# Splitting the operand waits of a three-pass matmul: high-high passes first, then low-high, then high-low

## The chip, the cores and the metric

The kernel runs on one NeuronCore of one Trainium2 chip. The metric is the device time of one execution in microseconds (us), the median of several runs. TensorE does the matmuls and has two sides in the profile: PE, the matmuls, and PEld, the loads of the stationary operand, which overlap them. VectorE is DVE, ScalarE is ACT, GpSimd is POOL, SyncE is SP.

## What is computed

The reference runs two decoder layers in float32 on `x` of 256 tokens by 1024 channels. Cut to what matters:

```python
for l in range(2):
    h = rmsnorm(x, norm_mix[l])
    qa, ka, va, qb, kb, vb, qi, ki, wi, qc, kc, vc, g = _split(h @ w_in[l], IN_SIZES)   # 1024 x 5316
    # three mixers: stick-breaking, top-k sparse, sliding window -> o_a, o_b, o_c
    merged = gates[..0] * (o_a @ w_pa[l]) + gates[..1] * (o_b @ w_pb[l]) + gates[..2] * (o_c @ w_pc[l])
    x = x + merged @ w_out[l]
    x = x + cross_attention(rmsnorm(x, norm_x[l]), rmsnorm(mem, norm_mem[l]),
                            w_xq[l], w_xkv[l], w_xo[l], qn_x[l], kn_x[l])
    hf = rmsnorm(x, norm_ffn[l])
    if l % 2 == 0: x = x + swiglu(hf, w_gu_dense[0], w_down_dense[0])         # 2816 wide
    else:          x = x + moe_swiglu(hf, w_router[0], w_gu_moe[0], w_down_moe[0])  # top 2 of 8, 3584 wide
```

Nearly all the arithmetic is in the products with weights.

## The kernel before

**Three passes.** A float32 operand is split in two float32r halves: the high half is a rounded copy made by ScalarE (`act_split` L379 for weights, `act_hi` L485 for activations), the low half the difference, made by VectorE (`dve_split` L385, `dve_lo` L492). A product `h @ w` is then hi x w_hi + lo x w_hi + hi x w_lo, three matmuls into the same PSUM bank. `pe_products` (L499) writes them out: for each 128-row chunk of the contraction, high-high (L504), low-high (L505), high-low (L506). Activations are stationary (128 x 128), weights stream (128 x 512).

**Slots.** Weights come in slots of 128 x 2048 numbers (1 MB; some have half of that), each loaded into one of three `raw` buffers, split by ScalarE into `w_hi` and by VectorE into `w_lo`, and read by TensorE. A slot of 4 chunks by 512 columns is 12 matmuls for each 128-row tile of activations; there are two row tiles in the layers and the dense part and one for an expert. A slot of the `pa` and `pb` projections has 2 chunks. Semaphores order it: `hi_done` and `lo_done` count the slots split, `mm_done` the slots that TensorE has finished. ScalarE waits for `mm_done` before it writes a `w_hi` buffer again, VectorE for `hi_done`, SyncE for `lo_done` before it loads into a `raw` buffer, and TensorE for `lo_done` at the start of each slot (L511, L603, L621, L731, L745). In the gate columns of the input projection the weights are used unsplit in float32 (`pe_gates`, L569).

**Activations.** Before a projection whose input is new (the memory, the normalised inputs "mix", "x" and "ffn", the merged rows "mrg"), TensorE transposes it (`pe_turn` L458), VectorE applies the gain (`dve_gain`, L482), ScalarE writes `hT_hi` (L490, semaphore `..._H`) and VectorE `hT_lo` (L495, `..._L`), each in two halves of 4 chunks. TensorE waits for `..._L` of a half before the slot that uses it (L534, L642, L763). The queue of each engine is in program order: VectorE drains a finished block out of PSUM (L1484, L945, L1664, L579) only after the low halves of up to three slots ahead (`ahead`, L413, and `dve_linear`, L537), where the program puts them first.

**Feed-forward.** The dense part has 11 chunks of 256 hidden channels, an expert has 14, and there are 8 experts, 112 expert chunks in all; both run in loops whose wait values are computed in registers. A chunk is two gate/up slots and one down slot. Between them ScalarE applies the SiLU, VectorE the product, TensorE transposes (L616, L716), ScalarE writes `aT_hi` (L683, L828) and VectorE `aT_lo` (L699, L893). The down slot waits for `lo_done` and for `aT_split`, which says that `aT_lo` is there (L621 and L622, L745 and L746). It has two output halves of 2 chunks each.

**Order of a layer on TensorE** (`pe_program`, L1156): memory keys, input projection, mixers with the gate columns in between, `pa`, `pb`, `pc`, merge, `out`, `xq`, cross attention, `xo`, feed-forward.

## Time and profile before

| | us |
|---|---|
| median of 3 runs (lowest to highest) | 1960.74 (1956.84 to 1961.72) |
| the profiled execution | 1955.1 |
| its span, first to last instruction | 1953.5 |
| busy: PE / PEld / DVE / ACT | 1754.0 / 1348.9 / 1377.2 / 1059.5 |
| L504, L505, L506 with hT, 1488 matmuls each | 610.6 / 597.3 / 596.6 busy |
| L504, L505, L506 with aT, 536 matmuls each | 213.6 / 212.7 / 212.7 busy |
| mean granted TensorE clock | 0.96 of full |

The busy times of PE are of overlapping matmuls whose ends are modelled; what counts is the distance between starts. The layers take the first 370 us and the stretch from 568 to 950, the dense part of layer 0 the time between, the experts the rest.

### The profile page before, as it was taken

To read this page: it belongs to the slowest core of one execution; us is meant where nothing else is said; L and a number is where in the kernel's file an instruction comes from. 1 tells how busy PE (TensorE), PEld (TensorE's weight loads), DVE (VectorE), ACT (ScalarE), POOL (GpSimd) and SP (SyncE) were. 2 spreads that over 40 slices of the span, in tenths; PEclk is the share of its full clock that TensorE was granted. 3 is DMA by queue.
4 is the path that set the end of the run, shared out by engine and by line. 5 is a ranking of instruction groups with operands and counts; after the bars stand their busy time and mean duration, and the time that the engine had idled before them with its cause. 6 is when DMAs were issued, how large, how long until landed. Compare 5 with 4: busy or idle time off the path is not lost.

```text
span 1953.5 us, 21775 instructions
## 1 busy us (share of the span) xinstructions
PE 1754.0 (90%) x7553; PEld 1348.9 (69%) x7553; DVE 1377.2 (70%) x1288; ACT 1059.5 (54%) x967; POOL 49.8 (3%) x69
## 2 busy tenths in 40 slices
PE   6796878799989968886499999999999999999995
PEld 5653466688867634665388887888888888888884
DVE  6447467554456464674488888888888888888884
ACT  4212434434343224243377777777777777777773
POOL 2100000000000000000100000000000000000000
PEclk9898989899989989897799999999999999999997
DMA  8821259255435312440699999999999999999993
GB/s 240 266 91 63 82 194 363 103 194 190 175 127 175 109 66 82 178 177 22 233 355 370 376 367 371 371 371 373 367 376 369 366 381 365 376 368 365 382 363 137
DMA packets 74813, 502.80 MB, mean 257 GB/s; under 512 B 8524, under 2 KB 9356, under 8 KB 18320
## 3 DMA queue, kind: packets, MB, share of 16 engines
q1 hardware_dynamic: 65712, 466.55, 62.6%
q0 software_dynamic: 8656, 34.57, 5.7%
q10 hardware_dynamic: 400, 1.08, 0.1%
q8 instruction: 28, 0.46, 0.1%
q14 instruction: 17, 0.14, 0.0%
HBM read 483.55 MB, written 18.61 MB: 257 GB/s over the span
## 4 chain that ended last, share of the span: by engine, by line
PE 76%; DVE 10%; ACT 6%; DMA 3%; issue 2%; DVEq 2%; POOL 0%; ACTq 0%; SPq 0%; POOLq 0%
PE ps L504 23%; PE ps L505 23%; PE ps L506 23%; DMA raw<-in_layer_tiles 3%; PE ps L569 2%; DVE w_lo L388 2%; PE ps L716 1%; ACT scratch L1259 1%; ACT w_hi L383 1%; DVE scratch L1386 1%; DVE st L1357 1%; DVEq L1360 1%; DVE scratch L1436 1%; DVE st L1440 1%; DVE hT_lo L495 1%
## 5 line engine op out<-in xcount | busy, mean ns | idle before, releaser
L504 PE MATMUL ps<-w_hi,hT_hi 128*128 128x512 f32 x1488 | 610.6, 410 | 57.9 <-DVE hT_lo L495 24.1
L505 PE MATMUL ps<-w_hi,hT_lo 128*128 128x512 f32 x1488 | 597.3, 401 | 0.0
L506 PE MATMUL ps<-w_lo,hT_hi 128*128 128x512 f32 x1488 | 596.6, 401 | 0.0
L884 DVE TENSOR_TENSOR w_lo<-raw,w_hi 128x2048 fp32r<-128x2048 f32 x168 | 385.0, 2292 | 69.4 <-ACT w_hi L820 69.4
L884 DVE TENSOR_TENSOR w_lo<-z,w_hi 128x2048 fp32r<-128x2048 f32 x168 | 384.5, 2290 | 51.7 <-ACT w_hi L820 48.6
L504 PEld LDWEIGHTS ps<-w_hi,hT_hi 128*128 128x128 f32 x1488 | 285.1, 192 | 130.4 <-DVE w_lo L388 30.0
L820 ACT ACTIVATE w_hi<-z 128x2048 fp32r<-128x2048 f32 x168 | 321.6, 1915 | 40.6 <-PE ps L506 34.7
L820 ACT ACTIVATE w_hi<-raw 128x2048 fp32r<-128x2048 f32 x168 | 321.0, 1911 | 24.3 <-PE ps L506 24.3
L506 PEld LDWEIGHTS ps<-w_lo,hT_hi 128*128 128x128 f32 x1488 | 285.3, 192 | 68.9
L505 PEld LDWEIGHTS ps<-w_hi,hT_lo 128*128 128x128 f32 x1488 | 285.6, 192 | 62.4
L388 DVE TENSOR_TENSOR w_lo<-raw,w_hi 128x2048 fp32r<-128x2048 f32 (+1 forms) x89 | 194.6, 2194 | 126.9 <-ACT w_hi L383 126.2
L383 ACT ACTIVATE w_hi<-raw 128x2048 fp32r<-128x2048 f32 (+1 forms) x89 | 162.6, 1834 | 199.7 <-PE ps L506 128.9
L504 PE MATMUL ps<-w_hi,aT_hi 128*128 128x512 f32 x536 | 213.6, 398 | 3.5 <-DVE aT_lo L893 2.0
L506 PE MATMUL ps<-w_lo,aT_hi 128*128 128x512 f32 x536 | 212.7, 397 | 0.0
L505 PE MATMUL ps<-w_hi,aT_lo 128*128 128x512 f32 x536 | 212.7, 397 | 0.0
L569 PE MATMUL ps<-raw 128*128 128x512 f32 (+1 forms) x384 | 158.4, 570 | 26.4 <-DVE z L579 26.4
L569 PEld LDWEIGHTS ps<-raw 128*128 128x128 f32 x384 | 72.7, 197 | 107.5 <-issue 107.2
L504 PEld LDWEIGHTS ps<-w_hi,aT_hi 128*128 128x128 f32 x536 | 100.9, 188 | 31.4 <-issue 5.5
L506 PEld LDWEIGHTS ps<-w_lo,aT_hi 128*128 128x128 f32 x536 | 101.1, 189 | 24.5
L505 PEld LDWEIGHTS ps<-w_hi,aT_lo 128*128 128x128 f32 x536 | 101.0, 188 | 23.7
L828 ACT ACTIVATE aT_hi<-ps 128x256 fp32r<-128x256 f32 x112 | 43.2, 385 | 107.9 <-PE ps L716 107.9
L824 ACT ACTIVATE headsT<-ps 128x256 f32<-128x256 f32 x112 | 42.9, 383 | 65.4 <-PE ps L506 65.4
(235 smaller groups left out, 1015.8 us busy)
## 6 DMA issues: line engine op xcount, KB each, us to landing
z<-in_moe_tiles SPq DMA_DIRECT2D x168, 1024.0 KB, 4.9
raw<-in_moe_tiles SPq DMA_DIRECT2D x168, 1024.0 KB, 4.8
raw<-in_layer_tiles SPq DMA_DIRECT2D x68, 1024.0 KB, 4.9
raw<-in_dense_tiles SPq DMA_DIRECT2D x33, 1024.0 KB, 4.8
rows_of_experts<-z POOLq DMA_DIRECT2D x1, 8704.0 KB, 44.2
z<-in_b_gate POOLq DMA_DIRECT2D x4, 1536.0 KB, 11.4
z<-rows_of_experts POOLq DMA_DIRECT2D x9, 512.0 KB, 8.2
raw<-in_layer_tiles SPq DMA_DIRECT2D x8, 512.0 KB, 3.9
```

Source lines behind the costliest of these rows:

```text
L383: act.activation(w_hi[:, ring, 0:width], raw[:, ring, 0:width], ACT.Copy).then_inc(sem("hi_done"), 1)
L388: v.tensor_tensor(w_lo[:, ring, 0:width], raw[:, ring, 0:width], w_hi[:, ring, 0:width].bitcast(F32), ALU.subtract).then_inc(sem("lo_done" ...
L495: v.tensor_tensor(hT_lo[:, ks, :], src[:, ks, :], hT_hi[:, ks, :].bitcast(F32), ALU.subtract) \
L504: pe.matmul(acc, a, wh, start=start and j == 0, stop=False)
L505: pe.matmul(acc, b, wh, start=False, stop=False)
L506: ins = pe.matmul(acc, a, wl, start=False, stop=stop and last)
L569: ins = pe.matmul(ps[:, LIN + i, 0:n], gate_x(l)[:, kk, i * P:(i + 1) * P], w[:, k, :], start=kk == 0, stop=kk == KC - 1)
L716: ins = pe.transpose(ps[:, 6, f * P:(f + 1) * P], a_sb[:, 0, f * P:(f + 1) * P], ident)
L820: act.activation(w_hi[:, ring, :], moe_raw(p), ACT.Copy).then_inc(sem("hi_done"), 1)
L824: act.activation(silu_sb[:, 0, :], ps[:, bank, 0:FC], ACT.Silu).then_inc(sem("silu"), 1)
L828: act.activation(aT_hi[:, :, 0:P], psA(1), ACT.Copy).then_inc(sem("aT_hi"), 1)
L884: v.tensor_tensor(w_lo[:, ring, :], moe_raw(p), w_hi[:, ring, :].bitcast(F32), ALU.subtract) \
```

## The change

`pe_products` runs all high-high passes of the chunks of a slot, then all low-high, then all high-low, for one row tile at a time. Two optional waits stand inside: `x_lo` (the low half of the activations) before the low-high passes and `w_lo_v` (`lo_done`) before the high-low ones. The callers pass them for the first row tile (or the first output half) of a slot alone. The waits at the start of a slot become waits for the high halves: `hi_done` for `lo_done`, `..._H` for `..._L`, `aT_hi` for `aT_split`. The waits for `oT_L` before `pa` and for `xo_L` before `xo` stay.

```diff
-        def pe_products(pe, acc, hk, wk, start, stop, hi=hT_hi, lo=hT_lo):
+        def pe_products(pe, acc, hk, wk, start, stop, hi=hT_hi, lo=hT_lo, x_lo=None, w_lo_v=None):
 
-            for j, ((k, cols), (wh, wl)) in enumerate(zip(hk, wk)):
-                a, b = hi[:, k, cols], lo[:, k, cols]
-                last = j == len(hk) - 1
-                pe.matmul(acc, a, wh, start=start and j == 0, stop=False)
-                pe.matmul(acc, b, wh, start=False, stop=False)
-                ins = pe.matmul(acc, a, wl, start=False, stop=stop and last)
+            for j, ((k, cols), (wh, _)) in enumerate(zip(hk, wk)):
+                pe.matmul(acc, hi[:, k, cols], wh, start=start and j == 0, stop=False)
+            if x_lo is not None:
+                pe.wait_ge(sem(x_lo[0]), x_lo[1])
+            for (k, cols), (wh, _) in zip(hk, wk):
+                pe.matmul(acc, lo[:, k, cols], wh, start=False, stop=False)
+            if w_lo_v is not None:
+                pe.wait_ge(sem("lo_done"), w_lo_v)
+            for j, ((k, cols), (_, wl)) in enumerate(zip(hk, wk)):
+                ins = pe.matmul(acc, hi[:, k, cols], wl, start=False, stop=stop and j == len(hk) - 1)
             return ins
 
-        def pe_block_slot(pe, ring, kcs, n, k0, lo_v, first, final, blk_v):
-
-            pe.wait_ge(sem("lo_done"), lo_v)
+        def pe_block_slot(pe, ring, kcs, n, k0, lo_v, first, final, blk_v, x_lo=None):
+
+            pe.wait_ge(sem("hi_done"), lo_v)
...
-                                  [(wh[:, k, :], wl[:, k, :]) for k in range(kcs)], first, final)
+                                  [(wh[:, k, :], wl[:, k, :]) for k in range(kcs)], first, final,
+                                  x_lo=x_lo if i == 0 else None, w_lo_v=lo_v if i == 0 else None)
...
+                    x_lo = None
                     if h_ready and b == b0:
-                        pe.wait_ge(sem(h_ready), 2 * l + h + 1)
+                        pe.wait_ge(sem(h_ready + "_H"), 2 * l + h + 1)
+                        x_lo = (h_ready + "_L", 2 * l + h + 1)
...
             def down(c, s, ring, first, last):
-                pe.wait_ge(sem("lo_done"), s + (1 - N_GATE))
-                pe.wait_ge(sem("aT_split"), c + 1)
+                pe.wait_ge(sem("hi_done"), s + (1 - N_GATE))
+                pe.wait_ge(sem("aT_hi"), c + 1)
...
-                                          hi=aT_hi, lo=aT_lo)
+                                          hi=aT_hi, lo=aT_lo, x_lo=("aT_split", c + 1) if i + h == 0 else None,
+                                          w_lo_v=s + (1 - N_GATE) if i + h == 0 else None)
...
-                pe.wait_ge(sem("ffn_L"), half + 1)
-                gate_up(0, half)
+                pe.wait_ge(sem("ffn_H"), half + 1)
+                gate_up(0, half, x_lo=("ffn_L", half + 1))
...
-        def pe_moe_gate_up(pe, par, k, ring, bank, lo_v):
-            pe.wait_ge(sem("lo_done"), lo_v)
+        def pe_moe_gate_up(pe, par, k, ring, bank, lo_v, x_lo=None):
+            pe.wait_ge(sem("hi_done"), lo_v)
...
-            pe.wait_ge(sem("hg_L"), n + 1)
+            pe.wait_ge(sem("hg_H"), n + 1)
```

The dense gate/up slots, the expert down slot and the calls of `pe_linear` for "mem", "mix", "mrg" and "x" are changed in the same way.

## Rows read from the trace of the kernel before

**Rows 1.** Page, part 4: the chain that ended last, by engine.
```profile
PE 76%; DVE 10%; ACT 6%; DMA 3%; issue 2%; DVEq 2%; POOL 0%; ACTq 0%; SPq 0%; POOLq 0%
```

**Rows 2.** Windows: stretch, length, busy us (instructions) of PE, PEld, DVE, ACT, POOL, granted clock, DMA.
```profile
965.30:1928.80 963.50, 961.50 (x4270) 773.25 (x4271) 841.25 (x563) 713.40 (x568) 7.46 (x14) 1.00 0.94 364
605.46:608.87 3.41, 3.41 (x9) 2.64 (x10) 1.43 (x5) 3.34 (x5) 0.00 (x0) 0.50 0.06 26
```

**Rows 3.** Timeline, a slot boundary in the expert loop: start us, us, engine, line.
```profile
1498.33 2.29 DVE L884 TENSOR_TENSOR w_lo<-raw,w_hi 128x2048 fp32r<-128x2048 f32 x1 [0.67 <-ACT w_hi L820]
...
1501.28 0.19 PEld L504 LDWEIGHTS ps<-w_hi,hT_hi 128*128 128x128 f32 x1
1501.51 0.40 PE L504 MATMUL ps<-w_hi,hT_hi 128*128 128x512 f32 x1
...
1501.74 0.40 PE L505 MATMUL ps<-w_hi,hT_lo 128*128 128x512 f32 x1
```

**Rows 4.** Timeline, second slot of `pa`, layer 0; brackets: idle before, releaser.
```profile
255.89 1.22 DVE L388 TENSOR_TENSOR w_lo<-raw,w_hi 128x1024 fp32r<-128x1024 f32 x1
...
257.17 0.69 PE L504 MATMUL ps<-w_hi,hT_hi 128*128 128x512 f32 x1 [2.10 <-DVE w_lo L388]
257.66 0.63 PE L505 MATMUL ps<-w_hi,hT_lo 128*128 128x512 f32 x1
258.08 0.63 PE L506 MATMUL ps<-w_lo,hT_hi 128*128 128x512 f32 x1
```

**Rows 5.** Chain in order of time, layer 0, start: start us, us, what.
```profile
40.32 22.80 DMA raw<-in_layer_tiles
```

**Rows 6.** Chain in order of time, first projections of layer 0.
```profile
263.93 4.75 DMA raw<-in_layer_tiles
```

**Rows 7.** Timeline of ACT and DVE, first projections of layer 0.
```profile
262.06 1.91 ACT L383 ACTIVATE w_hi<-raw 128x2048 fp32r<-128x2048 f32 x1 [3.04 <-DMA raw<-in_layer_tiles]
...
262.67 4.56 DVE L388 TENSOR_TENSOR w_lo<-raw,w_hi 128x1024 fp32r<-128x1024 f32 x3 [0.16 <-issue]
...
270.65 2.29 DVE L388 TENSOR_TENSOR w_lo<-raw,w_hi 128x2048 fp32r<-128x2048 f32 x1 [0.58 <-ACT w_hi L383]
```

**Rows 8.** Chain in order of time, output projection of layer 0.
```profile
299.33 4.49 DVE w_lo L388 x2
```

**Rows 9.** Timeline of DVE, drains of the query projection, layer 0 and layer 1.
```profile
333.66 0.75 DVE L1664 TENSOR_SCALAR scratch<-ps,st 128x512 f32<-128x512 f32 x1 [1.65 <-PE ps L506]
...
873.86 1.61 DVE L1664 TENSOR_SCALAR scratch<-ps,st 128x512 f32<-128x512 f32 x2
```

**Rows 10.** Timeline, start of the dense part, and input projection of layer 1.
```profile
371.25 2.36 DVE L495 TENSOR_TENSOR hT_lo<-scratch,hT_hi 128x1024 fp32r<-128x1024 f32 x2
...
372.53 0.50 PE L504 MATMUL ps<-w_hi,hT_hi 128*128 128x512 f32 x1 [2.72 <-DVE hT_lo L495]
...
605.29 0.67 PE L504 MATMUL ps<-w_hi,hT_hi 128*128 128x512 f32 x1 [2.40 <-DVE hT_lo L495]
```

**Rows 11.** Timeline of PE, start of the input projection of layer 0.
```profile
46.38 0.50 PE L504 MATMUL ps<-w_hi,hT_hi 128*128 128x512 f32 x1 [2.41 <-DVE hT_lo L495]
```

**Rows 12.** Timeline of PE, memory keys of layer 1 and first expert.
```profile
575.89 0.79 PE L504 MATMUL ps<-w_hi,hT_hi 128*128 128x512 f32 x1 [3.29 <-DVE hT_lo L495]
...
953.02 0.80 PE L504 MATMUL ps<-w_hi,hT_hi 128*128 128x512 f32 x1 [2.37 <-DVE hT_lo L898]
```

**Rows 13.** Timeline, second chunk of the first expert.
```profile
962.94 4.49 DVE L884 TENSOR_TENSOR w_lo<-raw,w_hi 128x2048 fp32r<-128x2048 f32 x2 [1.38 <-ACT w_hi L820]
...
965.29 0.50 PE L504 MATMUL ps<-w_hi,hT_hi 128*128 128x512 f32 x1 [1.58 <-DVE w_lo L884]
...
967.35 0.42 DVE L893 TENSOR_TENSOR aT_lo<-ps,aT_hi 128x256 fp32r<-128x256 f32 x1
```

**Rows 14.** Timeline, last down slot of the kernel.
```profile
1926.84 0.38 ACT L828 ACTIVATE aT_hi<-ps 128x256 fp32r<-128x256 f32 x1 [0.83 <-PE ps L716]
...
1928.82 0.48 PE L504 MATMUL ps<-w_hi,aT_hi 128*128 128x512 f32 x1 [2.01 <-DVE aT_lo L893]
```

More of the change, by code:

```diff
@@ L598, in pe_dense, with gate_up @@
         def pe_dense(pe, s0, n):
-            def gate_up(c, half):
+            def gate_up(c, half, x_lo=None):
                 s, ring = c * 3 + (s0 - 1 + half), place[s0 + 2 + half]
@@ L608, in gate_up @@
                     ins = pe_products(pe, ps[:, 4 + i, :], [(4 * half + k, cols) for k in range(4)],
-                                      [(wh[:, k, :], wl[:, k, :]) for k in range(4)], half == 0, half == 1)
+                                      [(wh[:, k, :], wl[:, k, :]) for k in range(4)], half == 0, half == 1,
+                                      x_lo=x_lo if i == 0 else None, w_lo_v=s + (1 - N_GATE) if i == 0 else None)
                 ins.then_inc(sem("mm_done"), 1)
@@ L717, in pe_turn_chunk, with pe_moe_down @@
             ins.then_inc(sem("aT_turned"), 1)
-        def pe_moe_down(pe, first, last, ring=None):
+        def pe_moe_down(pe, first, last, lo_v, aT_v, ring=None):
             ring = moe_ring(2) if ring is None else ring
+            pe.wait_ge(sem("hi_done"), lo_v)
+            pe.wait_ge(sem("aT_hi"), aT_v)
             wh = w_hi[:, ring, :].rearrange("p (k n) -> p k n", k=2)
@@ L726, in pe_moe_down @@
                                   [(wh[:, f, cols], wl[:, f, cols]) for f in range(2)], first, last,
-                                  hi=aT_hi, lo=aT_lo)
+                                  hi=aT_hi, lo=aT_lo, x_lo=("aT_split", aT_v) if h == 0 else None,
+                                  w_lo_v=lo_v if h == 0 else None)
             ins.then_inc(sem("mm_done"), 1)
-        def pe_moe_gate_up(pe, par, k, ring, bank, lo_v):
-            pe.wait_ge(sem("lo_done"), lo_v)
+        def pe_moe_gate_up(pe, par, k, ring, bank, lo_v, x_lo=None):
+            pe.wait_ge(sem("hi_done"), lo_v)
             wh = w_hi[:, ring, :].rearrange("p (k n) -> p k n", k=4)
@@ L734, in pe_moe_gate_up, with pe_moe_chunk @@
             pe_products(pe, ps[:, bank, :], [(4 * k + q, col_of(par)) for q in range(4)],
-                        [(wh[:, q, :], wl[:, q, :]) for q in range(4)], k == 0, k == 1).then_inc(sem("mm_done"), 1)
-        def pe_moe_chunk(pe, ip, par, u, d):
+                        [(wh[:, q, :], wl[:, q, :]) for q in range(4)], k == 0, k == 1, x_lo=x_lo, w_lo_v=lo_v) \
+                .then_inc(sem("mm_done"), 1)
+        def pe_moe_chunk(pe, ip, par, u, d, x_lo=None):
             off, coff, c = at(ip, par, MOE), at(ip, par, N_MOE), u * 2 + d
             static = isinstance(c, int)
-            pe_moe_gate_up(pe, par, 0, moe_ring(0), 4 + d, off + (u * 6 + (3 * d + SPL0)))
+            pe_moe_gate_up(pe, par, 0, moe_ring(0), 4 + d, off + (u * 6 + (3 * d + SPL0)), x_lo)
             pe.wait_ge(sem("act_done"), coff + (c + N_DENSE))
@@ L1169, in pe_program @@
                         .then_inc(sem("dist_ps"), 1)
-                pe_linear(pe, "xkv", l, nblk=1, h_ready="mem_L")
+                pe_linear(pe, "xkv", l, nblk=1, h_ready="mem")
                 if l == 0:
```

22 lines of the change are left out of this document (9 added, 13 removed).

## The prediction

> **What bounds the kernel now.** I read the shares of the chain that ended last first: 76% of it is TensorE, 10% VectorE, 3% a transfer [rows 1]. That share is not one thing, so the windows by stretch came next. From 965 to 1929 us, half of the run, TensorE is busy for 961.5 of 963.5 us at the full clock [rows 2]. There each matmul starts 0.23 us after the one before [rows 3], so a weight slot of 12 matmuls lasts 2.8 us, and the half that the change delays its wait for is ready early: one w_lo ends at 1500.62, and the slot that reads it starts its weight load at 1501.28 [rows 3]. TensorE is the bound, it waits for nothing, and the order of its passes leaves the number of its matmuls alone. The dense feed-forward of layer 0 looks the same. What the change can win lies in the rest, where the timeline shows TensorE standing before a matmul whose last releaser is a subtraction: hT_lo (L495, L898), w_lo (L388, L884) or aT_lo (L699, L893). I looked at each of these places for two things: when the high half was ready, and what comes after.
>
> **What a stall gives back.** TensorE now starts a slot when both halves of both operands are there. After the change it starts when the high halves are there, does 4 high-high matmuls (2 where the contraction has two chunks), then asks for the low half of the activations, does as many low-high ones, then asks for w_lo. Despite the change's title this runs one row tile at a time: only the passes of row tile 0 stand before the waits. So a stall on hT_lo is covered by at most 4 matmuls, 4 x 0.233 = 0.93 us at the full clock, or 1.7 us at half clock, where starts are 0.42 us apart [rows 4]; nor can more be won than the subtraction lasts. I now go through them in time.
>
> Layer 0, first 68 us (two stalls on hT_lo, the second before 46.38): nothing. The chain runs there through a weight transfer issued at 40.32 that takes 22.8 us [rows 5], and before it through ScalarE's and VectorE's own work.
>
> First projection after the mixers (once per layer): the second slot starts at 257.17 after 2.10 us idle, released by a w_lo that began, with w_hi done, at 255.89 [rows 4]. Two high-high and two low-high matmuls fit in the 1.28 us. They save 0.93 us at the full clock and up to 1.7 at half. That reaches the path: the drain of this slot, the next w_lo and the transfer issued at 263.93 hang on it [rows 6]. A cap comes from VectorE: the third of its next three subtractions needs a w_hi that ends at 262.06 + 1.91 = 263.97 (now it starts at 262.67 + 4.56 - 2.29 = 264.94), and the later w_lo at 270.65 has 0.58 us of idle before it [rows 7], so 0.97 + 0.58 = 1.55 us at most. I take 1.3 in each of two layers: **2.6**. The stall on w_lo before the slot behind it gives nothing: TensorE waits again later for drains that follow that transfer.
>
> Output projection (hT_lo, both layers): nothing. TensorE would start 0.93 us sooner, but the chain leaves it here: from hT_lo over the key statistics and the logarithm and exponential on ScalarE to two subtractions of 4.49 us [rows 8], behind which the drain of the finished block is queued on VectorE.
>
> Query projection (hT_lo): in layer 0 the last drain starts after 1.65 us of idle, in layer 1 the two drains run back to back, 1.61 us together [rows 9]; VectorE is the bound of the second to within 0.1 us. So **1.65** at most in layer 0, 0 in layer 1.
>
> Dense feed-forward, layer 0: hT_hi is ready at 371.25, TensorE starts at 372.53 [rows 10]: 0.93 saved. Layer 1, normalised input at 605.29: the same 0.93. Both stand in front of an unbroken run of TensorE.
>
> Clock. In four places a stall is followed by 3.41 us at a granted clock of 0.50 (one is shown, that of the layer-1 input, [rows 2]; the others are in the first projection, the query projection and the dense part of layer 0). In 3.41 us at 0.427 us apiece 8 matmuls start, which take 1.87 us at the full clock: a stretch costs 1.55 us. A stall with 0.9 us of work put into it may not bring the clock down; the one before 46.38, with 2.41 us idle, did not, for the first matmul after it lasts 0.50 us, not 0.69 as at 257.17 [rows 4, 11]. I count half, 0.77, for the dense and for the layer-1 input: **1.7 each**; the query projection's is in its 1.65.
>
> Memory keys of layer 1 (575.89, idle 3.29) and first expert (953.02, idle 2.37) start at half clock [rows 12]. hT_lo takes 1.22 us, all of which the high-high passes (1.7 us) fill. That is 1.2 us if the clock comes up as much sooner as TensorE starts, 1.2 x 0.233/0.427 = 0.66 if it comes up when it does now, and 2.8 if it comes up one such 3.41-us stretch sooner. I take **1.2** and **0.9**.
>
> First expert, 965.29: idle 1.58 us for a w_lo whose w_hi was done at 962.94 [rows 13]. The 8 matmuls ahead of the new wait (1.87 us) cover all of it, but the down slot behind it then meets aT_lo, which stands behind VectorE's two subtractions of 4.49 us and ends at 967.77 [rows 13]. TensorE would start at 965.29 - 1.58 = 963.71, reach that slot at 966.5, do its 2 high-high matmuls and wait; then 10 matmuls from 967.8 end 0.8 us sooner than 12 from 963.71 + 1.58 + 2.9 = 968.2 do now: **0.8**.
>
> aT_lo before the last down slot of the dense part and of the kernel: 2 high-high matmuls fit in between aT_hi, at the second done at 1926.84 + 0.38 = 1927.22, and the start at 1928.82 [rows 14]: **0.9** for both.
>
> Sum: 2.6 + 1.65 + 1.7 + 1.7 + 1.2 + 0.9 + 0.8 + 0.9 = 11.5 us. With every term at its lower bound (1.9 + 0.9 + 0.9 + 0.9 + 0.7 + 0.7 + 0 + 0.9) it is 6.9, at its upper (3.1 + 1.65 + 2.5 + 2.5 + 2.8 + 1.3 + 1.6 + 0.9) 16.4. The profiled execution took 1955.1 us around a span of 1953.5, so it would take 1943.6. The median of the runs is 5.6 us above that execution, and I take the gain off the median: 1960.7 - 11.5 = **1949.2 us**.
>
> **What it adds.** One more wait on TensorE per weight slot, two more in a down slot (for the two halves of aT), and the arithmetic for their values in the loops. Queued behind each is only TensorE's own stream; ScalarE waits for its end to reuse w_hi, SyncE for VectorE's subtractions, whose order is unchanged. No DMA moves. A slot already begins with a wait, and a met one shows no gap: 1501.28, 1501.51, 1501.74 run on at 0.23 across the boundary [rows 3]. The new wait for w_lo stands 8 matmuls later (1.87 us), so it is met 0.66 + 1.87 = 2.5 us ahead. I cost it at zero; the cover is this lead. The Trainium skill ("TensorE: Matmul & The Clock Gate", section "Step-by-step: what each phase is for") has weight loads pulled ahead of the matmuls in flight. By that the sum stays as it is as long as a met wait doesn't stop it, of which the page says nothing; if it did, each new wait would lay a load bare, which is the second rival. Below zero isn't possible, since TensorE's rate in the expert loop is that of its matmuls. The bound above zero is that rival's 45 to 85 us.
>
> **Rivals.** (1) *The saved time is lost downstream.* Twice above VectorE's fixed chain already took all of it. If that also holds in the layer-1 input, the query projection and the first projection, what is left is dense, aT, memory and expert starts at their lower bounds: 0.9 + 0.9 + 0.7 + 0.7 = 3.2 us, 1957.5 us. For: VectorE is in nearly every chain of the layers. Against: in the timeline it idles for TensorE at those places. (2) *A wait inside the stream costs although it is met*: the next weight load can't be started under the matmul before. The loads take 0.19 us and start one matmul ahead [rows 3]; the first matmul after a stall lasts 0.50 instead of 0.40 [rows 3, 13], so 0.10 each is exposed. There are 112 expert chunks (8 experts by 14), with 4 waits inside the slots of each (two gate/up slots one each, the down slot two): 448 x 0.10 = 45 us, less 11, gives 1994 us, and with the full 0.19 load 2034. It decides as soon as TensorE's instruction stream is read less than one matmul ahead. For it: no row of before has a wait between two passes of a slot. Against: the present waits at slot starts, also in front of a weight load, show none of it. (3) *The clock helps everywhere*: no half-clock stretch is left after any stall, and the starts come a step sooner: the upper sum, 16 us or a little more, 1943 us. (4) The order is what the diff says, but the waits are met in the same order as before because ACT's high half is late rather than VectorE's low half: excluded, since at each stall above the high half is earlier by at least its subtraction's 0.4 to 2.3 us.
>
> **How the numbers follow.** Forecast 1949 (6.9 to 14 us won): 0.66. Rival 3: 0.12. Rival 1: 0.17. Rival 2: 0.05. What a measurement of this kernel can tell from no change is about 0.3%, 5.9 us. Faster by more: the forecast, rival 3 and a little of rival 1, 0.79; within it: the rest of rival 1, 0.16; slower 0.05. The range for 8 in 10 takes in rival 3 and the better part of rival 1: 1941 to 1957.
>
> **What would show it.** Right: L504 starts released by ACT hT_hi or w_hi at the stalls, L505 (low-high) by DVE hT_lo with about 0.3 us of idle, the expert stretch of 963.5 us the same to within 1, and the same starts 0.23 us apart. Shorter stalls with the drains at the old distance would show rival 1; starts over 0.23 apart at a change of pass inside the expert loop, rival 2. The prediction is wrong at its root if the expert stretch changes at all by more than its first 3 us.

## The result, and the profile after

The changed kernel took 1938.8 us (median of 4 runs, 1937.5 to 1940.4) beside 1961.2 us of the kernel before (4 runs, 1956.8 to 1962.0): a ratio of 0.989, 95% interval 0.9874 to 0.9905. The forecast was 1949.2 us with a range of 1941 to 1957. The sign was right and the size was not: the time is outside the range by 2 us. Run again with more executions beside it, the change took 1937.6 against 1956.9 us, ratio 0.9895 [0.9880, 0.9909], so 19 to 22 us. In these medians one execution of each kernel, of some 3550 us, is left out as slow. The four runs of before on record lie high, for the same kernel had medians of 1956.7 to 1956.9 us in four later sessions.

The profiled execution of after took 1940.4 us around a span of 1938.7; that of before 1955.1 around 1953.5. The two traces differ by 14.8 us, and that difference is what can be followed row by row. It is less than that of the medians, because the profiled execution of after was the slowest of its four and that of before was quicker than all four of its runs. Line numbers have moved: the three passes are now L502 (high-high), L506 (low-high) and L510 (high-low). First the page of after: the shares of its chain, and the three passes with the idle time just before them.

```profile
PE 76%; DVE 10%; ACT 6%; DMA 3%; issue 2%; DVEq 2%; POOL 0%; ACTq 0%; SPq 0%; POOLq 0%
...
L502 PE MATMUL ps<-w_hi,hT_hi 128*128 128x512 f32 x1488 | 426.8, 408 | 42.2 <-DVE z L586 13.2
L506 PE MATMUL ps<-w_hi,hT_lo 128*128 128x512 f32 x1488 | 414.9, 400 | 1.4 <-DVE hT_lo L495 0.9
L510 PE MATMUL ps<-w_lo,hT_hi 128*128 128x512 f32 x1488 | 413.2, 399 | 3.2 <-DVE w_lo L388 3.2
```

The shares are the same as in [rows 1]; they don't show the change at all. The idle times do: in front of the low-high pass with hT 1.4 us are left in the whole kernel (and 1.5 with aT), in front of the high-low pass 3.2. The busy column can't be set beside that of before: it counts overlapping matmuls of one line once, and in after four matmuls of one line follow each other. The mean length of one matmul, 408, 400 and 399 ns, is within 2 ns of before's 410, 401 and 401. The waits of TensorE say what this replaced. Of the kernel before (in its second profiled execution, span 1953.3), the rows with a subtraction's result as the releaser; columns are total us, times, longest:

```profile
PE ps L504 <- DVE hT_lo L495: 23.1, 11, 3.5
PE ps L504 <- DVE w_lo L388: 8.5, 4, 2.2
PE ps L504 <- DVE hT_lo L898: 2.4, 1, 2.4
PE ps L504 <- DVE aT_lo L893: 2.0, 1, 2.0
PE ps L504 <- DVE w_lo L884: 1.6, 1, 1.6
PE ps L504 <- DVE aT_lo L699: 1.5, 1, 1.5
```

The same view of after, every row of the three passes with a half of an operand as the releaser:

```profile
PE ps L502 <- ACT hT_hi L490: 10.0, 9, 2.6
PE ps L510 <- DVE w_lo L388: 3.2, 4, 1.2
PE ps L502 <- DVE hT_lo L495: 2.8, 2, 1.4
PE ps L506 <- DVE aT_lo L902: 1.5, 2, 0.8
PE ps L502 <- ACT hT_hi L841: 1.1, 1, 1.1
PE ps L502 <- ACT w_hi L383: 1.1, 2, 0.6
PE ps L506 <- DVE hT_lo L495: 0.9, 1, 0.9
PE ps L502 <- ACT aT_hi L692: 0.8, 1, 0.8
PE ps L502 <- ACT aT_hi L837: 0.6, 1, 0.6
```

Before, these waits sum to 39.1 us; after, to 22.0. That is 17.1 us less. All waits of TensorE together fell from 178.8 to 164.7 us, 14.1 less, while the span fell by 14.6: over the whole kernel nearly all of the gain is idle time of TensorE, and 3.0 us of the 17.1 came back in front of other matmuls. The busy time is 1753.5 us, and it was 1754.5. This balance holds for the sum only: in single stages the time in matmuls changed by up to 5 us, in both directions, through the clock.

The expert loop, which the prediction called full, became a little shorter, and the waits in it cost nothing. Windows of after from the second chunk of the first expert to the last down slot, then a stretch in the layer-1 input and one in the output projection of layer 0 (columns as in [rows 2]), and in the fence after it the timeline of TensorE over one gate/up slot inside the loop and the turn behind it:

```profile
953.08:1914.81 961.73, 960.32 (x4273) 774.35 (x4272) 841.86 (x563) 715.21 (x570) 7.47 (x14) 1.00 0.94 364
599.24:602.65 3.41, 3.35 (x15) 2.41 (x14) 2.00 (x2) 3.33 (x4) 0.00 (x0) 1.00 0.42 178
302.50:305.91 3.41, 3.41 (x10) 2.62 (x9) 3.11 (x14) 0.00 (x0) 0.00 (x0) 0.50 1.04 437
```

```profile
1324.08 1.09 PE L502 MATMUL ps<-w_hi,hT_hi 128*128 128x512 f32 x4
1325.02 1.09 PE L506 MATMUL ps<-w_hi,hT_lo 128*128 128x512 f32 x4
1325.95 1.09 PE L510 MATMUL ps<-w_lo,hT_hi 128*128 128x512 f32 x4
1326.88 0.38 PE L725 MATMUL ps<-consts,headsT 128*128 128x128 f32 x2
```

The stretch of [rows 2] lasted 963.5 us and lasts 961.7: 1.4 us less between its second chunk and the last turn, 1.4 less in the wait that ends it, and 1.1 more at its start, where TensorE now comes early and waits for aT_lo. The passes follow each other after 0.94, 0.93 and 0.93 us, four matmuls of 0.233 us each, although a wait stands between the second and the third. From 966.6 us to the last turn, all 874 changes of pass in the expert loop, half of them with a wait, are 0.230 to 0.235 us from the start before. In the layer-1 input the granted clock is 1.00 where it was 0.50; in the output projection of layer 0 a stretch at 0.50 stands where before had none.

The places of the sum, in the timeline of after, in order of time: TensorE's first high-high matmul at the dense part, at the memory keys of layer 1 and at the layer-1 input; VectorE's last drains of the query projection of layer 1; the first expert; the last down slot:

```profile
371.43 0.50 PE L502 MATMUL ps<-w_hi,hT_hi 128*128 128x512 f32 x1 [1.46 <-ACT hT_hi L490]
...
571.80 1.80 PE L502 MATMUL ps<-w_hi,hT_hi 128*128 128x512 f32 x4 [2.59 <-ACT hT_hi L490]
...
598.90 1.20 PE L502 MATMUL ps<-w_hi,hT_hi 128*128 128x512 f32 x4 [1.15 <-ACT hT_hi L490]
...
863.33 1.41 DVE L1673 TENSOR_SCALAR scratch<-ps,st 128x512 f32<-128x512 f32 x2
...
941.86 2.07 PE L502 MATMUL ps<-w_hi,hT_hi 128*128 128x512 f32 x4 [1.11 <-ACT hT_hi L841]
...
1916.16 0.74 PE L506 MATMUL ps<-w_hi,aT_lo 128*128 128x512 f32 x2 [0.65 <-DVE aT_lo L902]
```

The idle times of [rows 10, 12] are 0.7 to 1.3 us shorter and are now ended by ScalarE's high half: 2.72 became 1.46, 3.29 became 2.59, 2.40 became 1.15, 2.37 became 1.11. The last row shows where the new order is not enough: two high-high matmuls of a down slot don't fill the time that aT_lo takes, and 0.65 us are left.

### The profile page after: what moved, and what is told of

The parts are those of the page before. It is cut to its first block, busy times and chain, and to the rows that moved or that the text cites. A ratio compares the mean times of both kernels' runs of the same rounds, so it can differ in the third digit from the quotient of the medians.

```text
span 1938.7 us, 21775 instructions
## 1 busy us (share of the span) xinstructions
PE 1753.5 (90%) x7553; PEld 1346.2 (69%) x7553; DVE 1377.0 (71%) x1288; ACT 1059.6 (55%) x967; POOL 49.8 (3%) x69
## 4 chain that ended last, share of the span: by engine, by line
PE 76%; DVE 10%; ACT 6%; DMA 3%; issue 2%; DVEq 2%; POOL 0%; ACTq 0%; SPq 0%; POOLq 0%
PE ps L506 23%; PE ps L510 23%; PE ps L502 23%; DMA raw<-in_layer_tiles 3%; DVE w_lo L388 2%; PE ps L576 2%; PE ps L725 1%; ACT w_hi L383 1%; ACT scratch L1268 1%; DVE scratch L1395 1%; DVE st L1366 1%; PE ps L1160 1%; DVEq L1369 1%; DVE scratch L1445 1%; DVE st L1449 1%
## 5 line engine op out<-in xcount | busy, mean ns | idle before, releaser
L502 PE MATMUL ps<-w_hi,hT_hi 128*128 128x512 f32 x1488 | 426.8, 408 | 42.2 <-DVE z L586 13.2
L506 PE MATMUL ps<-w_hi,hT_lo 128*128 128x512 f32 x1488 | 414.9, 400 | 1.4 <-DVE hT_lo L495 0.9
L510 PE MATMUL ps<-w_lo,hT_hi 128*128 128x512 f32 x1488 | 413.2, 399 | 3.2 <-DVE w_lo L388 3.2
L502 PEld LDWEIGHTS ps<-w_hi,hT_hi 128*128 128x128 f32 x1488 | 271.7, 191 | 105.1 <-issue 22.6
L510 PEld LDWEIGHTS ps<-w_lo,hT_hi 128*128 128x128 f32 x1488 | 282.7, 190 | 73.6 <-DVE w_lo L388 4.9
L506 PEld LDWEIGHTS ps<-w_hi,hT_lo 128*128 128x128 f32 x1488 | 282.5, 190 | 72.9 <-DVE hT_lo L495 5.3
L506 PE MATMUL ps<-w_hi,aT_lo 128*128 128x512 f32 x536 | 168.7, 396 | 1.5 <-DVE aT_lo L902 1.5
L502 PE MATMUL ps<-w_hi,aT_hi 128*128 128x512 f32 x536 | 168.5, 396 | 1.3 <-ACT aT_hi L692 0.8
L510 PE MATMUL ps<-w_lo,aT_hi 128*128 128x512 f32 x536 | 168.4, 396 | 0.0
L506 PEld LDWEIGHTS ps<-w_hi,aT_lo 128*128 128x128 f32 x536 | 100.5, 188 | 26.8 <-DVE aT_lo L902 2.4
L502 PEld LDWEIGHTS ps<-w_hi,aT_hi 128*128 128x128 f32 x536 | 100.5, 188 | 26.0 <-issue 1.8
L510 PEld LDWEIGHTS ps<-w_lo,aT_hi 128*128 128x128 f32 x536 | 100.7, 188 | 24.4
```

The source lines that it names most:

```text
L502: pe.matmul(acc, hi[:, k, cols], wh, start=start and j == 0, stop=False)
L506: pe.matmul(acc, lo[:, k, cols], wh, start=False, stop=False)
L510: ins = pe.matmul(acc, hi[:, k, cols], wl, start=False, stop=stop and j == len(hk) - 1)
```

## The experiments

All ran beside the kernel before on the same chip; a ratio is to those runs. The first four shared 28 runs of before (median 1956.8 us), the next four 16 (1956.9), the next four 21 (1956.8), the last two 23 (1956.7). A gain "by the ratio" is the ratio's share of that median; it differs from the difference of the medians by up to 1.7 us.

**The kernel before again.** No edit.

> The kernel before, unchanged, for a second profile and more times. The change took 22.4 us off the median but only 14.8 us between the two profiled executions, since the profiled one of before (1955.1 us) lay 6 us under the median of its runs. Theory A (the profiled execution of before was a quick one, and executions of one kernel differ by some us through the half-clock stretches of TensorE): ratio 1.000, and a profile of 1957 to 1962 us whose extra time against the first lies in matmul runs at half clock in the two layers, with the expert loop the same to 1 us. Theory B (profiling itself makes before quicker): this profile is again at 1955 us, 5 us or more under the median.

1954.9 us, 12 runs from 1952.8 to 1960.9, ratio 0.9999 [0.9985, 1.0012]. Neither theory came out as written: the profile was again at 1954.9 us, but this time that is the median of its runs. What follows: executions of one kernel lie 8 us apart here, and the 88 of before in the four sessions 11 us (1951.8 to 1962.6), while their work is the same. So a single profile is not the kernel's time, and gains below 3 us are read from many runs or not at all.

**The order alone.** All waits in front of the first pass.

```diff
+            if w_lo_v is not None:
+                pe.wait_ge(sem("lo_done"), w_lo_v)
+            if x_lo is not None:
+                pe.wait_ge(sem(x_lo[0]), x_lo[1])
             for j, ((k, cols), (wh, _)) in enumerate(zip(hk, wk)):
                 pe.matmul(acc, hi[:, k, cols], wh, start=start and j == 0, stop=False)
-            if x_lo is not None:
-                pe.wait_ge(sem(x_lo[0]), x_lo[1])
```

> The pass order of the change (high-high, low-high, high-low), with all waits back in front of the first pass: for both high halves, then the low half of the activations, then that of the weights. Theory A (only the shortened stalls give time, the order costs and gives nothing): 1961 us within 3, ratio 0.998 to 1.002, starts 0.233 us apart in the expert loop. Rival C (the order itself is quicker, for instance at the 112 transposes of the expert loop, whose stretch drifted by 1.4 us between the two profiles): 1 to 8 us quicker than before without any split wait.

1959.1 us (12 runs), ratio 1.0013 [0.9999, 1.0027]: nothing, or up to 5 us lost. The order alone gains nothing, so the gain is in the places of the waits. (This kernel also has one more wait in front of a slot than before; what that does in the expert loop is told further down.)

**The activations' low half late, w_lo early**, and the reverse. In each, one of the two waits stands between the passes and the other in front of them.

> The change with the wait for w_lo back in front of the first pass: only the wait for the low half of the activations (hT_lo, aT_lo) stands between passes. Theory A by its terms: dense 0.9 to 2.5, layer-1 input 0.9 to 2.5, memory 0.7 to 2.8, query projection up to 1.65, first expert 0.9, aT_lo 0.9: 7 us off 1961, so 1954. The prediction under-sized the memory and input terms of layer 1 (4.6 us between the profiles where 2.9 was said), so up to 10 us: 1951 to 1954. Rival D (the w_lo splits give most of the gain): 1956 or more.

1946.0 us (6 runs), ratio 0.9942 [0.9925, 0.9959], 11.4 us by the ratio.

> The change with the wait for the low half of the activations back in front of the first pass: only the wait for w_lo stands between passes. Theory A: first projections (pa to pc) 3.0 us in each of two layers as the profile of after shows there, second chunk of the first expert 0.8 to 1.8: 7 to 8 us off 1961, so 1953 to 1954. With the split of the activations' wait 14 to 18 us in sum, so that the two halves add up to the whole change within 3 us. Rival D (w_lo splits give most): 1945 or less.

1949.6 us (11 runs), ratio 0.9968 [0.9955, 0.9980], 6.3 us by the ratio. Both kernels were faster than what was expected of them, some 4 us of which is that the expectations started from 1961 us. Both halves of the change work by themselves and nearly add up to the whole. The prediction had 3.4 us for the w_lo places (2.6 and 0.8) and 8.1 for the rest; the runs give about 6 and 11. Both parts were sized too small.

**The change again.**

> The change, unchanged, for its ratio with many more runs of both kernels: 28 later runs of before had a median of 1956.8 us, not 1961.2, and the activation split alone gave 11, the weight split alone 7 us. Theory A (the two splits add up, and the 22.4 us of the first comparison held some 4 us of spread of before): 1938 to 1941 us, ratio 0.990 to 0.992. Theory B (the first comparison was right, and the two splits together give more than their sum): 0.989 or less.

1937.6 us, ratio 0.9895 [0.9880, 0.9909]. The gain holds: 19.2 us by the medians, 20.5 by the ratio.

**Unused matmuls in two idle times of the kernel before**, 3.4 us of them in front of the first wait for the activations in the input blocks of layer 1 and in the dense part. No pass is moved.

```diff
+        def pe_fill(pe, bank, n):
+            for _ in range(n):
+                pe.matmul(ps[:, bank, :], ident, consts[:, 0:4, :].rearrange("p i n -> p (i n)"), start=True, stop=True)
...
+                        if name == "in" and l == 1 and h == 0:
+                            pe_fill(pe, 5, 4)
...
+                if half == 0:
+                    pe_fill(pe, 6, 4)
                 pe.wait_ge(sem("ffn_L"), half + 1)
```

> The kernel before, with waits and pass order as they were, and with matmuls added whose results nothing reads: 4 (identity by constants, float32, 128x512, 0.427 us apart at the full clock) in front of the wait of the layer-1 input projection, and 4 in front of the dense part's first wait. They only fill idle time of TensorE. Theory K (half of what a covered stall gives is the half-clock stretch after it, 1.55 us each, which work inside the idle time avoids): the stretches of 3.41 us at half clock from 373 and 605 us are gone and the dense part and the input projection end 1.55 us sooner each: 3 us off, ratio 0.9984 give or take the interval. Theory N (the clock has no part in it, the low-high order hides work only): no change or slower by the added work, 0 to +1 us at these two places.

1956.5 us (12 runs), ratio 0.9992 [0.9983, 1.0001]. Each of these float32 matmuls is two instructions of 0.427 us, 3.4 us in all, where the idle times are 2.7 and 2.4: the filling ends 0.7 to 1 us behind the operand. It cost TensorE that time, and the kernel was no slower, which suggests that something of that size came back. The stretch at half clock at 605 us was gone, the one at 373 stood 12 us later. Since two effects cancel here, the size was set right in a later run.

**Unused matmuls in three longer waits of after** (8.5 us ahead of the first wait of the cross attention, 15.4 us behind the product for the top-k, 4.3 us in the output projection).

> The change plus unused matmuls of the same kind in three long waits of TensorE in each layer: 5 before the second output-projection block, 10 before the wait for the cross-attention probabilities, 18 before the gate columns that wait for the drain during the top-k. Theory K: the half-clock stretches that start in these waits vanish (in the profile of after: 302 in layer 0, 343 and 876 of 10 us, part of 169 and 705), each us of matmuls that ran at half clock costs 0.45 us: 4 to 10 us off the change, 1930 to 1936. Theory N: 1939 or slower, since nothing is gained and a filler that overruns its wait delays the chain.

1946.4 us (6 runs), ratio 0.9950 [0.9934, 0.9966], 9 us slower than after. The granted clock of the profiled execution was the highest of all (0.925 to 0.976 over the six):

```profile
die 0 (median of its cores): 1942.4 us, clock 0.976
```

That is 0.976 where after had 0.96, in a longer span: behind each of the six groups of fillers the next matmul starts with no idle time before it, so the fillers, longer than the waits, stood in the path. A clock that is up is no gain if the way to keep it up stands in the path.

**All row tiles first.** In slots that aren't the last of their block, and in the first dense slot, the high-high pass of both row tiles, then low-high of both, then high-low of both. This is what the change's title says and its code does not.

```diff
+            for acc, hk in zip(accs, hks):
+                for j, ((k, cols), (wh, _)) in enumerate(zip(hk, wk)):
+                    pe.matmul(acc, hT_hi[:, k, cols], wh, start=start and j == 0, stop=False)
+            if x_lo is not None:
+                pe.wait_ge(sem(x_lo[0]), x_lo[1])
+            for acc, hk in zip(accs, hks):
+                for (k, cols), (wh, _) in zip(hk, wk):
+                    pe.matmul(acc, hT_lo[:, k, cols], wh, start=False, stop=False)
+            pe.wait_ge(sem("lo_done"), w_lo_v)
```

> The change as its title says it: in every slot that is not the last of its block (and in the first dense gate/up slot) the high-high passes of both row tiles stand before the low-high passes of both, and those before the high-low ones, so 8 high-high matmuls (1.9 us) stand in front of the wait for hT_lo instead of 4 (0.93 us). hT_lo takes 1.22 us, so each full-clock stall is covered for all of it: 0.3 us more at each of five places (dense, layer-1 input, query projection of layer 0; the memory and output ones give nothing more). Theory A: 1 us off the change, 1938 us within 2. Rival: the second tile's drain wait now stands before all passes, and the slots give back 0.3 to 1 us each: 1940 to 1945.

1950.0 us (5 runs), ratio 0.9956 [0.9943, 0.9969]: 12 us slower than after. The waits of TensorE of this kernel that grew, for the drain of the input blocks, the memory keys and the first projections:

```profile
PE ps L517 <- DVE z L611: 15.7, 8, 9.2
PE ps L517 <- DVE mem_kv L1671: 3.4, 1, 3.4
PE ps L502 <- DVE scratch L1524: 8.9, 4, 3.3
```

A block whose first pass runs over both tiles needs both drains of the previous block before it starts, and VectorE does them one after the other: 8 waits for z instead of 3. In after these rows have 13.2, 0.5 and 7.0 us, 7.3 less together, of the 11.1 us by which the two profiles differ. Row tile by row tile, the second drain is hidden behind the first tile's 12 matmuls.

**Only pa, pb and pc.** The kernel before, with the new order and the late wait for w_lo in these three blocks alone; and its opposite, after with the wait for w_lo in front of the first pass there.

```diff
+            pe.wait_ge(sem("hi_done" if split else "lo_done"), lo_v)
...
+                if split:
+                    ins = pe_products_split(pe, ps[:, LIN + i, 0:n], hk, wk, first, final, lo_v if i == 0 else None)
```

> The kernel before with one part of the change alone: in the blocks pa, pb and pc of both layers TensorE waits for the high half of the weights in front of the first pass and for w_lo in front of the high-low pass, in the new order; everywhere else the code is that of before. The prediction put this part at 2.6 us in all, since VectorE's drain was taken for the cap (1.55 us a layer, 1.3 used). The profiles of before and after show 3.2 and 3.0 us a layer between the start of pa and the end of pc. Theory A (the transfer one slot earlier sets the stage, the cap was wrong, and it is this part alone that does it): 5 to 7 us faster than before, ratio 0.9965 to 0.9975, and in the profile 3.0 us less from the start of pa to merge in each layer, of which some 1.55 us is a stretch at the low clock that is no longer there. Theory B (the prediction's term was right and the rest comes from elsewhere in the change): 2 to 3.5 us faster, ratio about 0.9985.

1950.6 us (10 runs), ratio 0.9970 [0.9959, 0.9980], 5.9 us faster.

> The change without that part: the kernel after, but in pa, pb and pc the wait for w_lo stands in front of the first pass again; all else is after. Theory A of the run before (6 us belong to this part and the parts add up): 1944 to 1946 us beside 1957 of before, ratio 0.9935. Theory B (the part is worth 2.6 us): 1940 to 1941.5, ratio about 0.991.

1943.4 us (6 runs), ratio 0.9933 [0.9916, 0.9950], slower than after by 5.7 us by the medians of the two sessions, 7.4 by the ratios. Both say the same thing from either side: 6 to 7 us for the two layers, where the prediction had 2.6. TensorE's waits for w_lo there, first with the late wait, then without:

```profile
PE ps L508 <- DVE w_lo L388: 3.0, 4, 1.2
```

```profile
PE ps L502 <- DVE w_lo L388: 8.5, 4, 2.2
```

**Fillers that fit.** As above, 1.7 us at each of the two places of before.

> The kernel before with unused float32 matmuls that fit into two waits, 1.7 us each (four instructions of 0.427 us), in front of the first wait for the activations in the input blocks of layer 1 and in the dense layer; the idle times there were 2.4 and 2.7 us, so nothing is overrun. No pass is moved. Theory A (what the change takes from the low clock at these places is a saving of its own, one stretch of 3.41 us at half clock, worth some 1.55 us, for each idle time that gets too short): the stretches at 372 and 605 us are gone and the kernel is 1.5 to 3 us faster than before, ratio 0.9985 to 0.9992. Theory B (the stretches only move to the next short wait): the same as before within 0.5 us, and new stretches at half clock show behind the filled waits.

1954.0 us (12 runs), ratio 0.9980 [0.9969, 0.9992]: 2.8 us by the medians, 1.6 to 6.1 by the interval, faster without a pass or a wait moved. The start of the dense part, in this kernel's timeline:

```profile
372.68 1.88 PE L461 MATMUL ps<-consts 128*128 128x512 f32 x4
375.56 0.50 PE L509 MATMUL ps<-w_hi,hT_hi 128*128 128x512 f32 x1 [1.00 <-DVE hT_lo L500]
375.90 0.40 PE L510 MATMUL ps<-w_hi,hT_lo 128*128 128x512 f32 x1
```

The row behind the first is 0.34 us later, at the full clock. In the kernel before (its second profile) the layer-1 input began like this, with the next row 0.59 us later and then 0.42 us apiece:

```profile
605.49 0.80 PE L504 MATMUL ps<-w_hi,hT_hi 128*128 128x512 f32 x1 [2.41 <-DVE hT_lo L495]
606.08 0.63 PE L505 MATMUL ps<-w_hi,hT_lo 128*128 128x512 f32 x1
606.50 0.63 PE L506 MATMUL ps<-w_lo,hT_hi 128*128 128x512 f32 x1
```

The stretch at half clock behind the wait of the layer-1 input, there in both profiles of before, is gone with fillers and gone with the change, which shortens this idle time by 1.3 us. Over all kernels of this section and both profiles of before and after it is the same: the stretch is there in all six profiles in which this wait stands as before (starting between 601.5 and 606.2 us), and in none of the ten in which the wait is late or filled. The one at the dense part is in the first profile of before and not in the second; of that place alone the profiles prove nothing. At the layer-1 input the stretch is a cost beside the idle time, and an idle time that TensorE partly works through doesn't bring it on.

**Fillers that fit, in the three longer waits of after** (1.7, 4.3 and 7.7 us).

> The kernel after with unused float32 matmuls in three longer waits of each layer, now sized to the idle time: 1.7 us in front of the second output block, 4.3 us in front of the first wait of the cross attention, 7.7 us after the product that is sent to the top-k. Nothing of the computation is changed. Theory A (a stretch at half clock behind a long wait is avoided by keeping TensorE at work in the wait, 1.5 to 3 us each, and the earlier attempt lost only by overrunning the waits): 4 to 9 us faster than after, 1930 to 1935 us beside 1957 of before. Theory B (the time behind these waits is set by VectorE or a transfer, not by TensorE's clock): the same as after within 1 us, 1937 to 1939. Theory C (it still overruns): slower than after, 1940 or more.

1942.5 us (6 runs), ratio 0.9924 [0.9910, 0.9939], still 5 us slower than after: theory C by the number, though not by its reason, for behind each of the six groups of fillers TensorE is idle for 0.4 to 1.5 us more. Its granted clock in the profile:

```profile
die 0 (median of its cores): 1942.5 us, clock 0.964
```

The second profile of after has the same 0.964; over all executions this kernel had 0.964 to 0.969 and after 0.960 to 0.964, so the clock came up by little. Beside that profile of after the time is lost in the mixers with the fillers of the top-k, 3.0 us in layer 0 and 4.2 in layer 1; in layer 0 three stretches at half clock (from 186, 204 and 217 us) stand there that it has not. Another 1.4 us are lost by 74 us, ahead of any filler; behind the other fillers 1.6 and 0.8 us are won in layer 0. Why the stretches came there isn't known. None of the kernels tried beats after.

**The activations' low half late, in two groups.** From the third kernel of this section: first only in layer 1's memory and input blocks and in the dense part, then everywhere else.

```diff
+                        if l == 1 and h_ready in ("mem", "mix"):
                             pe.wait_ge(sem(h_ready + "_H"), 2 * l + h + 1)
                             x_lo = (h_ready + "_L", 2 * l + h + 1)
+                        else:
+                            pe.wait_ge(sem(h_ready + "_L"), 2 * l + h + 1)
```

> The kernel before with the new pass order, and with the wait for the activations' low half late in two groups only: the memory and input blocks of layer 1 and the first two slots of the dense layer. Every other wait stands as before. The prediction's terms for these are 1.2, 1.7 and 1.7 us, 4.6 in all. Theory A (the excess is the half-clock stretches that these idle times bring on): 6 to 7.5 us faster than before, ratio 0.9962 to 0.9969, with no stretch at half clock at 605 us. Theory B (the excess is elsewhere): 4 to 5 us, ratio about 0.9977.

1951.4 us (12 runs), ratio 0.9974 [0.9961, 0.9986], 5.3 us faster than before.

> The complement of the run before: the new pass order, the wait for the activations' low half late in the memory and input blocks of layer 0, the output and query projections of both layers, the starts of the experts and everywhere the gated activation's two halves are used; the memory and input blocks of layer 1, the dense layer's first slots and all waits for w_lo as before. The prediction's terms for these sum to 3.5 us (1.65 query of layer 0, 0.9 start, 0.9 halves). Theory A (these terms were right): 3 to 4.5 us faster than before, ratio 0.9977 to 0.9985, the stretch at half clock at 605 us still there. Theory B: 5 us or more, ratio under 0.9975.

1956.6 us (12 runs from 1947.6 to 1959.8), ratio 0.9998 [0.9985, 1.0010]: no faster than before. The first is nearer to theory B, though the stretch at 605 us is gone as theory A says; the second is below both theories, nothing where 3.5 us were predicted. Its profiled execution is the fastest of its 12, 9 us under their median, so its trace does not stand for its runs. Together the two groups give some 5.5 us, and the whole late wait for the activations gave 11: the parts don't add up, and why isn't shown.

## Why the prediction was off

**What held.** TensorE's rate at the full clock didn't change, the gain over the whole kernel is idle time before matmuls whose last releaser was a subtraction, and a wait that is met costs nothing: rival 2 falls, with the starts 0.23 us apart at every change of pass in the loop. The Trainium skill ("TensorE: Matmul & The Clock Gate", section "Step-by-step: what each phase is for") has weight loads pulled ahead of the matmuls in flight; the trace agrees also with a met wait between them (the load at 948.99 us, its matmul at 949.22, the matmul before them at 948.99), of which the page says nothing. Rival 1 falls for the kernel as a whole: only 3.0 of 17.1 us came back as other waits. The prediction's own sign for the expert stretch, the same to within 1 us, was missed by 0.8 (963.5 and 961.7).

**Place by place**, the difference of the two profiles (what the start of the next stage moved by), with the forecast in brackets: query projection of layer 0 1.7 us (1.65) and of layer 1 0.2 (0; VectorE's drains run back to back in both, [rows 9] and 863.33 above), first expert's second chunk 0.7 (0.8), output projections 0 but for the clock (0). Memory keys of layer 1 2.1 (1.2), layer-1 input 2.5 (1.7), dense part 2.5 (1.7), end of the kernel 2.3 (0.45), down slot of the dense part 0.7 (0.45), first projections 3.2 and 3.0 (1.3 each), expert loop 1.4 (0), start of the first expert 0.3 (0.9). Against them stand losses that no step had: 1.6 us in the output projection of layer 0 and 2.9 and 0.7 in the cross attentions, through half-clock stretches that fell elsewhere, and 0.7 ahead of the first projection. The sum is 14.7, of the profiles' 14.8.

**The step that failed: the half-clock stretches of the first projections, put at nothing.** The prediction saw that TensorE could start 0.9 to 1.7 us sooner there, limited the gain to 1.55 us a layer by VectorE's next subtractions, took 1.3, and added nothing for the clock. Its paragraph on the clock names one stretch at half clock in this stage of layer 0; before had three of them in it in each layer (from 257.3, 264.1 and 274.4 us, and from 800.0, 806.9 and 817.1), and after has one in layer 0 (268.4) and two, one behind the other, in layer 1 (800.8 to 807.7). The waits did what they should (rows of TensorE in the second slot of pa):

```profile
256.42 0.74 PE L502 MATMUL ps<-w_hi,hT_hi 128*128 128x512 f32 x2 [0.58 <-ACT w_hi L383]
257.00 0.63 PE L506 MATMUL ps<-w_hi,hT_lo 128*128 128x512 f32 x2
257.95 0.73 PE L510 MATMUL ps<-w_lo,hT_hi 128*128 128x512 f32 x2 [0.32 <-DVE w_lo L388]
```

Here is the stage from the first matmul of pa to the last of pc, layer 0 and layer 1, first of before, then of after (columns as in [rows 2]; the length less PE's busy time is TensorE's idle time):

```profile
252.03:286.67 34.64, 28.03 (x96) 21.16 (x96) 24.69 (x26) 11.88 (x8) 0.00 (x0) 0.85 0.65 231
794.62:829.28 34.66, 28.03 (x96) 21.10 (x96) 24.69 (x26) 11.99 (x8) 0.00 (x0) 0.85 0.62 229
```

```profile
252.81:284.13 31.32, 25.45 (x96) 18.68 (x96) 24.54 (x26) 11.90 (x8) 0.00 (x0) 0.95 0.70 253
787.01:818.72 31.71, 26.32 (x96) 19.59 (x96) 24.64 (x26) 12.00 (x8) 0.00 (x0) 0.89 0.70 251
```

The idle time fell from 6.6 to 5.9 us and from 6.6 to 5.4: 0.7 and 1.2 us, 2.0 in all, so the cap of 1.55 held and the 2.6 were even a little much. TensorE's waits for w_lo fell by more, from 8.5 to 3.2 us, and the rest of that came back in front of drains and of w_hi: in this stage rival 1 holds in part. The other 4.3 of the 6.3 us are the same 192 matmuls at a higher clock, which had no term. The second profiles of before and after show the same split. The runs with these blocks alone and without them put the part at 6 to 7 us.

How much of this belongs to the late wait? The other kernels show that the stage moves in steps of the stretches. With w_lo asked for in front of the first pass it lasted 34.6 to 34.8 us in ten of 18 cases (nine profiles, two layers each; three stretches), 33.0 to 33.2 in three (two stretches), 31.5 to 31.7 in four (one stretch), and 32.8 in one. With the late wait it lasted 31.2 to 31.7 us in 13 of 14, and 32.7 in the kernel with all row tiles first. One of the four is layer 0 of the first kernel with unused matmuls, whose code up to this point is that of before, pass order and all, since its first filler comes later:

```profile
251.17:282.67 31.50, 25.02 (x96) 18.46 (x96) 24.63 (x26) 11.91 (x8) 0.00 (x0) 0.95 0.70 253
```

It has 6.5 us of idle time, nearly as much as before, and is 3.1 us shorter all the same; the second kernel with unused matmuls, with the same code up to here, took 34.8. So with one stretch in either the late wait is worth 0.2 to 0.3 us in layer 0, and most of its gain in this stage is that the long cases stay away. That the shorter idle times are what keeps them away fits the layer-1 input above, but was not tried in this stage.

**The second: the clock was counted at half.** The terms of the dense part and the layer-1 input had 0.77 us of a possible 1.55 each. Neither stretch is in the profiles of after, and fillers that fit were worth 2.8 us (1.6 to 6.1) at the two places, where 3.1 is two whole stretches and 1.5 was predicted; the interval leaves out 1.5 by a hair only. At the end of the kernel, where before had a stretch at half clock from 1929.8 us on, after has none. Rival 3, which said so everywhere, had too small a number for it and was also not quite right: other stretches appeared, as the one at 302.50.

**The third: the loop was not quite full.** The prediction put nothing on it. In the kernel before (second profile) the down slot of some chunks waits some hundredths of a us for an aT_lo:

```profile
1332.45 0.42 DVE L893 TENSOR_TENSOR aT_lo<-ps,aT_hi 128x256 fp32r<-128x256 f32 x1
...
1332.99 0.45 PE L504 MATMUL ps<-w_hi,aT_hi 128*128 128x512 f32 x1
```

Here aT_lo ends at 1332.87 and the slot begins at 1332.99. 16 of the 112 chunks last 8.65 to 8.79 us instead of 8.61; in after none does. That fits aT_lo being asked for two matmuls later, and is 1.4 us over the loop. With the order alone these chunks last 8.80 to 8.91 us and the loop 2.1 us longer than before. It is not the order that does this: the two last kernels have the same order, and their loops are 0.1 and 1.2 us shorter than that of before. The order alone has four waits in front of a down slot, before and these two have fewer there; that this is the reason is not shown.

**What stays open.** The two groups of the activations' wait give 5 to 6 us less than the whole of it, more than the half width of any one interval (2.4 to 3.3 us). And with w_lo's 6.3 and the activations' 11.4 the whole should be 17.7 us; it is 19.2 by the medians of its second session and 20.5 by the ratio, about the width of the intervals. In the cross attention of layer 0 TensorE was 2.5 us less idle and 5.4 us longer in its matmuls; why the stretches fell there is not known. How the half-clock stretches fall in an execution was not under control in any run.

## What to carry to other kernels

Where an operand comes in two halves and the product in three passes, ask for each half only in front of the pass that reads it, and keep the passes row tile by row tile: that took 17 us off the waits for operands and cost nothing in the full stretches. A cap worked out from another engine's starts bounds the idle time of TensorE and says nothing of its clock: list every stretch at half clock in the stage, each with its price, before the stage gets its term. Here an idle time of 2 to 3 us in front of TensorE cost itself plus, often, 1.5 us of half clock behind it. Check a few executions before a single profile's stretches are put down to a change.

## What the runs showed of the hardware

By the spacing of the starts, 0.427 against 0.233 us, a stretch of 3.41 us at half clock costs an estimated 1.55 us if TensorE has matmuls to do in it, and one stage of this kernel did come in lengths of 34.6, 33.1 and 31.6 us with three, two and one of them. Where such stretches fall differs between executions of one kernel (the one at 373 us is in one profile of before and not in the other). The times of one kernel spread over 8 us in 12 runs (1952.8 to 1960.9) and 11 us in 88. How much of that is the clock isn't shown: executions of before with the same mean clock of 0.958 took 1951.8 to 1961.5 us. A float32 matmul of 128x512 went through TensorE as two instructions of 0.427 us each, where one pass of the kernel's own kind starts every 0.233 us.
